# One decoder layer on one core: value products placed next to scores, the last token tile finished in two column halves, the first unit multiplied in order of arrival, stores from two queues

## What is computed

```python
h = rms_norm(x, norm_mix)
cols = h @ w_in                        # 9752 columns: q, k, v of three attentions, and gates
y_a = swa_attention(...)               # window 128, sinks, 8 heads of 64
y_b = stick_breaking(...)              # 4 heads of 128
y_c = nsa_attention(...)               # compressed, selected and window branches, 8 heads of 64
merged = sum(sigmoid(g_i) * (y_i @ w_br_i) for i in (a, b, c))
x = x + merged @ w_out
h = rms_norm(x, norm_ffn)
x = x + (silu(h @ w_gate) * (h @ w_up)) @ w_down    # inner width 5632
out = rms_norm(x, norm_final)
```

## Time and profile before

| | |
|---|---|
| median of three executions | 1398.5 us |
| the profiled execution's own time | 1400.08 us |
| its span | 1398.4 us |
| granted clock of TensorE, mean | 0.998 |
| PE matmul busy | 1386.4 us, 99% |
| PE weight loads busy | 1172.5 us, 84% |
| DVE, ACT, POOL busy | 66%, 50%, 3% |
| DMA | 260.58 MB, 186 GB/s |

### The profile page before, as it was taken

How to read it: one execution, slowest core, us unless ns; L and a number is a source line. 1 busy time by engine, 2 the same in 40 slices (tenths; PEclk the granted TensorE clock), 3 DMA queues, 4 the chain that set the end, 5 groups by cost and what they waited for, 6 DMA issues and landing times.

```text
span 1398.4 us, 18555 instructions
## 1 busy us (share of the span) xinstructions
PE 1386.4 (99%) x7344; PEld 1172.5 (84%) x7344; DVE 923.2 (66%) x1189; ACT 701.9 (50%) x912; POOL 45.4 (3%) x70
## 2 busy tenths in 40 slices
PE   9999999999999999999999999999999999999997
PEld 8999977777788888888888989888888898888886
DVE  5455557657655657666788888874446788887554
ACT  7333356656545655465645555543334455545443
POOL 4000000000000110000000000000000000000111
PEclk9999999999999999999999999999999999999999
DMA  7777755545565667556566665565666575667653
GB/s 239 247 217 219 216 140 150 149 139 148 150 184 164 188 200 213 174 164 201 157 182 204 213 184 177 184 216 193 191 185 179 182 221 164 192 190 228 207 188 115
DMA packets 135233, 260.58 MB, mean 186 GB/s; under 512 B 8448, under 2 KB 25408, under 8 KB 134768
## 3 DMA queue, kind: packets, MB, share of 16 engines
q1 hardware_dynamic: 133328, 251.89, 59.7%
q0 software_dynamic: 1792, 7.57, 1.5%
q10 hardware_dynamic: 32, 0.01, 0.0%
HBM read 257.33 MB, written 2.10 MB: 186 GB/s over the span
## 4 chain that ended last, share of the span: by engine, by line
PE 94%; DVE 3%; DMA 1%; ACT 1%; issue 1%; SPq 0%; ACTq 0%; DVEq 0%
PE bank L628 25%; PE bank L629 25%; PE bank L630 25%; PE bank L867 5%; PE bank L869 5%; PE bank L870 5%; PE bank L619 2%; DVE weight_lo_ring L1259 1%; DMA raw_ring<-in_w_up 1%; PE bank L766 1%; PE bank L677 1%; DVE weight_sums_lo L1279 0%; ACT weight_hi_ring L1029 0%; DMA x<-in_x 0%; DVE weight_sums L1268 0%
## 5 line engine op out<-in xcount | busy, mean ns | idle before, releaser
L1259 DVE TENSOR_TENSOR weight_lo_ring<-raw_ring,weight_hi_ring 128x1024 fp32r<-128x1024 f32 (+2 forms) x480 | 581.3, 1220 | 326.6 <-ACT weight_hi_ring L1029 273.0
L1029 ACT ACTIVATE weight_hi_ring<-raw_ring 128x1024 fp32r<-128x1024 f32 (+2 forms) x432 | 448.7, 1051 | 363.4 <-PE bank L630 297.2
L628 PE MATMUL bank<-weight_hi_ring,hT_hi 128*128 128x512 f32 (+2 forms) x768 | 303.3, 395 | 0.0
L629 PE MATMUL bank<-weight_lo_ring,hT_hi 128*128 128x512 f32 (+2 forms) x768 | 296.9, 387 | 0.0
L630 PE MATMUL bank<-weight_hi_ring,hT_lo 128*128 128x512 f32 (+2 forms) x768 | 296.8, 386 | 0.0
L628 PEld LDWEIGHTS bank<-weight_hi_ring,hT_hi 128*128 128x128 f32 x768 | 145.0, 189 | 31.2 <-issue 6.5
L630 PEld LDWEIGHTS bank<-weight_hi_ring,hT_lo 128*128 128x128 f32 x768 | 145.0, 189 | 27.2
L629 PEld LDWEIGHTS bank<-weight_lo_ring,hT_hi 128*128 128x128 f32 x768 | 145.2, 189 | 24.6
L628 PE MATMUL bank<-weight_hi_ring,h2T_hi 128*128 128x512 f32 x352 | 139.6, 397 | 0.6 <-DVE weight_lo_ring L1259 0.5
L629 PE MATMUL bank<-weight_lo_ring,h2T_hi 128*128 128x512 f32 x352 | 139.1, 395 | 0.0
L628 PE MATMUL bank<-weight_hi_ring,actT_hi 128*128 128x512 f32 x352 | 139.0, 395 | 0.0
(11 more groups left out here) (238 smaller groups left out, 1736.5 us busy)
## 6 DMA issues: line engine op xcount, KB each, us to landing
raw_ring<-in_w_in SPq DMA_DIRECT2D x96, 512.0 KB, 3.6
raw_ring<-in_w_gate SPq DMA_DIRECT2D x88, 512.0 KB, 4.5
raw_ring<-in_w_up SPq DMA_DIRECT2D x88, 512.0 KB, 4.3
raw_ring<-in_w_down SPq DMA_DIRECT2D x88, 512.0 KB, 4.6
raw_ring<-in_w_in SPq DMA_DIRECT2D x56, 452.0 KB, 4.2
raw_ring<-in_w_out SPq DMA_DIRECT2D x32, 512.0 KB, 4.6
raw_ring<-in_w_br_c SPq DMA_DIRECT2D x16, 256.0 KB, 4.7
raw_ring<-in_w_br_a SPq DMA_DIRECT2D x16, 256.0 KB, 7.4
```

The costliest lines, as they stand in the source:

```text
L628: pe.matmul(dst, x_hi, w_hi, start=first and k == 0, stop=False)
L629: pe.matmul(dst, x_hi, w_lo, start=False, stop=False)
L1029: act.activation(whi[:, s, :, 0:width(u)], raw[:, s, :, 0:width(u)], ACT.Copy).then_inc(hi_ready, 1)
L1259: dve.tensor_tensor(lo, w, hi.bitcast(F32), ALU.subtract).then_inc(lo_ready, 1)
```

## The change

Four edits stand in one diff.

- `VALUES_AT` is the scores' slot + 6 instead of + 7, on PE and DVE.
- In the last chunk, tile 1 is multiplied in two halves of 256 columns, each in a bank of its own (3 and 6), in all ten units. In the last four units the order is tile 0, first half of tile 1, second half of tile 1. DVE adds each half by itself, and ACT squares each by itself into its own column of `sumsq`.
- ACT stores the chunks that it scales from its own DMA queue; SP stores those of DVE.
- Unit 0 is multiplied as four high-by-high matmuls, four with the low weights, four with the low activations, each group with its own wait. ACT and DVE take the weights of unit 0 before the transposed piece.

```diff
-VALUES_AT = {soft_slot(i) + 7: i for i in range(N_SOFT)}
+VALUES_AT = {soft_slot(i) + 6: i for i in range(N_SOFT)}
...
             for t in range(TT):
-                for n in range(NC_D // 2):
-                    for name, c in (("dve", DVE_OUT[t][n]), ("act", ACT_OUT[t][n])):
-                        sp.wait_ge(scaled[name], t * NC_D // 2 + n + 1)
-                        sp.dma_start(out_b[:, t, c * W:(c + 1) * W], X[:, t, c * W:(c + 1) * W]).then_inc(stored, 16)
+                for n, c in enumerate(DVE_OUT[t]):
+                    sp.wait_ge(scaled["dve"], t * NC_D // 2 + n + 1)
+                    sp.dma_start(out_b[:, t, c * W:(c + 1) * W], X[:, t, c * W:(c + 1) * W]).then_inc(stored, 16)
...
+            def first_unit():
+
+                pe.wait_ge(t_hi, 1)
+                pe.wait_ge(hi_ready, 1)
+                for r, (x, w) in enumerate(((hT_hi, whi), (hT_hi, wlo), (hT_lo, whi))):
+                    if r == 1:
+                        pe.wait_ge(lo_ready, 1)
+                    if r == 2:
+                        pe.wait_ge(t_lo, 1)
+                    for k in range(UK):
+                        for t in range(TT):
+                            m = pe.matmul(bank[t][:, 0:WQ], x[:, k, t * P:(t + 1) * P], w[:, 0, k, 0:WQ],
+                                          start=r == 0 and k == 0, stop=False)
+                m.then_inc(unit_used, 1)
...
+                    if i == LAST_DOWN:
+                        products(u % RING, (actT_hi, actT_lo), c % 2, j == 0, False, UK * j, tiles=(0,))
+                        for e in range(2):
+                            m = half_products(u, j, e)
+                        m.then_inc(unit_used, 1)
+                        return
...
+            def half_products(u, j, e):
+
+                dst = bank[LAST_HALF[e]][:, 0:Q4]
+                last = j == KD_H[1] - 1
+                for k in range(UK):
+                    x_hi, x_lo = (m[:, UK * j + k, P:S] for m in (actT_hi, actT_lo))
+                    w_hi, w_lo = quarters(u, k, e)
+                    pe.matmul(dst, x_hi, w_hi, start=j == 0 and k == 0, stop=False)
+                    pe.matmul(dst, x_hi, w_lo, start=False, stop=False)
+                    m = pe.matmul(dst, x_lo, w_hi, start=False, stop=last and k == UK - 1)
+                return m
+
             def last_units():
 
                 n = KD_H[1]
-                for t in range(TT):
+                for j in range(n - RING, n):
+                    u = AT["down", LAST_DOWN, j]
+                    pe.wait_ge(lo_ready, u + 1)
+                    m = products(u % RING, (actT_hi, actT_lo), LAST_DOWN[1] % 2, False, j == n - 1, UK * j, tiles=(0,))
+                m.then_inc(tile0_full, 1)
+                for e in range(2):
                     for j in range(n - RING, n):
...
+                        m = half_products(AT["down", LAST_DOWN, j], j, e)
+                        if e == 1:
                             m.then_inc(unit_used, 1)
...
+                    if e == 0:
+                        m.then_inc(last_half_full, 1)
...
             for m in range(UPC):
+                if m == 0:
+                    split(m)
                 hi_of_transposed(m, 4 + m % 4, hT_hi[:, 2 * m:2 * m + 2, :], gainT[:, 0, 2 * m:2 * m + 2])
-                split(m)
+                if m > 0:
+                    split(m)
...
+                for e in range(1 + t):
+                    act.wait_ge(added, TT * (NC_D + c) + t + e + 1)
+                    act.wait_ge(squares, 2 * TT * NC_D + TT * c + t + e)
+                    w = W // (1 + t)
+                    act.activation(bank[7][:, 0:w], X[:, t, c * W + e * w:c * W + (e + 1) * w], ACT.Square,
+                                   accum_out=sumsq[:, t, c + e:c + e + 1]).then_inc(squares, 1)
                 root(3 + t, slice(t, t + 1))
...
+                    act.activation(X[:, t, cols], X[:, t, cols], ACT.Copy, scale=rstd[:, t:t + 1]).then_inc(scaled["act"], 1)
+                    act.wait_ge(scaled["act"], t * NC_D // 2 + n + 1)
+                    act.dma_start(out_b[:, t, cols], X[:, t, cols]).then_inc(stored, 16)
...
+                if (h, c) == LAST_DOWN:
+                    dve.wait_ge(tile0_full, 1)
+                    dve.tensor_tensor(X[:, 0, cols], bank[2 * (c % 2)][:, :], X[:, 0, cols], ALU.add).then_inc(added, 1)
+                    finish(0)
+                    for e in range(2):
+                        dve.wait_ge(last_half_full, 1) if e == 0 else dve.wait_ge(unit_used, v + 1)
+                        half = slice(c * W + e * Q4, c * W + (e + 1) * Q4)
+                        dve.tensor_tensor(X[:, 1, half], bank[LAST_HALF[e]][:, 0:Q4], X[:, 1, half],
+                                          ALU.add).then_inc(added, 1)
+                    finish(1)
+                    return
```

More of the change, by code:

```diff
@@ L121 @@
 LAST_DOWN = (1, NC_D - 1)
+LAST_HALF = (3, 6)
 def is_seven(u):
@@ L253, in build_layer @@
         gainT = place("gains_T", [4, KD])
-        sumsq = place("sumsq", [TT, NC_D])
+        sumsq = place("sumsq", [TT, NC_D + 1])
         stat = place("stat", [6, TT])
@@ L1239, in _ @@
             for t in range(TT):
-                act.wait_ge(added, TT * (NC_D + c) + t + 1)
-                square(t, c, bank[7], 2 * TT * NC_D + TT * c + t)
+                for e in range(1 + t):
[4 more added lines that the diff above has]
+                                   accum_out=sumsq[:, t, c + e:c + e + 1]).then_inc(squares, 1)
                 root(3 + t, slice(t, t + 1))
                 act.wait_ge(rstd_ready, 3 + t)
-                for n in ACT_OUT[t]:
-                    act.wait_ge(gained, n + 1)
-                    piece = X[:, t, n * W:(n + 1) * W]
-                    act.activation(piece, piece, ACT.Copy, scale=rstd[:, t:t + 1]).then_inc(scaled["act"], 1)
+                for n, chunk in enumerate(ACT_OUT[t]):
+                    act.wait_ge(gained, chunk + 1)
+                    cols = slice(chunk * W, (chunk + 1) * W)
+                    act.activation(X[:, t, cols], X[:, t, cols], ACT.Copy, scale=rstd[:, t:t + 1]).then_inc(scaled["act"], 1)
+                    act.wait_ge(scaled["act"], t * NC_D // 2 + n + 1)
+                    act.dma_start(out_b[:, t, cols], X[:, t, cols]).then_inc(stored, 16)
         @block.vector
@@ L1332, in add_down @@
                 cols = slice(c * W, (c + 1) * W)
+                if (h, c) == LAST_DOWN:
[8 more added lines that the diff above has]
+                    finish(1)
+                    return
+                dve.wait_ge(unit_used, v + 1)
                 for t in range(TT):
-                    if (h, c) == LAST_DOWN and t == 0:
-                        dve.wait_ge(tile0_full, 1)
-                    else:
-                        dve.wait_ge(unit_used, v + 1)
                     dve.tensor_tensor(X[:, t, cols], bank[2 * (c % 2) + t][:, :], X[:, t, cols], ALU.add).then_inc(added, 1)
-                    if (h, c) == LAST_DOWN:
-                        finish(t)
             def finish(t):
-                norm(3 + t, 3 * TT * NC_D - TT + t + 1, slice(t, t + 1))
+                norm(3 + t, 3 * TT * NC_D - TT + 2 * t + 1, slice(t, t + 1))
                 dve.wait_ge(rstd_ready, 3 + t)
@@ L1373, in norm @@
                 total, mean, root, y, z = (stat[:, r, tiles] for r in (2, 0, 1, 3, 4))
-                chain(dve.tensor_reduce(out=total, in_=sumsq[:, tiles, :], axis=AX_X, op=ALU.add))
+                n_sums = NC_D + (tiles == slice(1, TT))
+                chain(dve.tensor_reduce(out=total, in_=sumsq[:, tiles, 0:n_sums], axis=AX_X, op=ALU.add))
                 dve.tensor_scalar(mean, total, 1.0 / D, EPS, ALU.mult, ALU.add).then_inc(mean_ready, 1)
```

11 lines of the change are left out of this document (3 added, 8 removed).

## The result

The changed kernel took 1401.49 us (median of 22 executions, 1399.71 to 1403.55), the kernel before 1398.62 us (22 executions, 1397.45 to 1400.74). The ratio is 1.0019, with a 95% interval of 1.0012 to 1.0026: 2.9 us slower, where 1396.4 had been forecast and the range ended at 1398.2.

A forecast was written before the change was run, and what follows sets the result against it. PE was taken as the bound, busy 99% of the span. Values -1.7, start -0.05, halves +0.1 -0.5 and stores +0.1 sum to -2.05 us, from a median of 1398.5 to 1396.4; range 1394.8 to 1398.2.

The forecast's parts named there:

- the rivals: Four cases for the time: middle as summed (chance 0.64), free change of form (0.17), no middle gain (0.14), ACT's queue (0.05).
- ACT's queue: Rival in the tail: slow store issues on ACT make the kernel slower, 1399.9 at an issue of 1.4 us; chance 0.05.
- Values next to scores: Attention stretch on PE: joining eight value groups to scores saves 0.20 us each; with the compressed values -1.7 us, range 0 to 3.3.
- The compressed group: Full-width compressed values in attention, behind scores: they save the scores' return alone, 0.11 us.
- The first unit: Start of PE's work: unit 0 waits for less, but PE's filler queue hides most of it; -0.05 us.
- The 0.11 us at most: Upper bound on the gain before unit 0: last filler started at 8.63, first matmul at 8.74.
- the rate of the first unit's matmuls changes at another time: One of the signs, to be read in the changed profile, that would show the prediction wrong.
- Two halves: Last chunk: 120 matmuls of 256 columns replace 60 of 512, +0.1 us on PE; shorter tail, -0.49; net -0.4.
- The tail: After PE's last matmul: DVE's add 0.69 to 0.42 us, ACT's square 0.60 to 0.38, together -0.49.
- Stores: Last stores from two queues: SP's 0.5 us of queueing goes, but ACT's issue of 0.46 delays its second scaling; +0.1 us.
- no store landed more than 3.5 us after issue: Sign at the end: the last store landing more than 3.5 us after its issue would show the prediction wrong; 3.3 was assumed.

## Why the prediction was wrong

- **The step that failed** is the list of what the change adds. The prediction priced matmuls, adds, squares, waits and stores, and gave the ninth column of `sumsq` no term. It moved the activations by 32 bytes against the weights and cost 5.3 us (1401.49 against 1396.20), twice all that the four edits win. None of the rivals had it either; the one that ended slower, ACT's queue, did not occur. Every price per matmul was taken from rows of before and assumed to hold after; with the addresses moved it did not.
- **Values next to scores** was right: -1.7 predicted, -1.75 measured alone, one change of form per pair (2.33 us for the joined group against 2.32). Scores to values cost what scores to a unit cost: the 0.85 us from the first score to the first value product is the 0.85 from the first score to L628 in the earlier trace rows. "Mode switching requires drain", the Trainium skill says (TensorEngine Tiling (Array Packing), Key Properties). The trace agrees that this change is not free; its size comes from the rows alone. The compressed group saved nothing where 0.11 was assumed.
- **The first unit** was mis-sized: -0.05 predicted, -0.7 measured alone (with an interval up to +0.6). The 0.11 us at most was read from one execution with slow fillers. In an execution where they are fast, PE reached unit 0 earlier than 8.63 and waited; "the rate of the first unit's matmuls changes at another time" was named as what would show the prediction wrong, and it did, but as a gain. It also hid the loss: the profiled execution of after had this 3.0 us head start.
- **Two halves** was mis-sized on PE: from the first matmul of the last chunk to the last is 27.65 us before and 28.11 with the old addresses restored. With the last matmul's own 0.23 and 0.12 that is +0.34, not +0.1: the halves step at 0.118 to 0.119 rather than 0.117, and the rest, under 0.1, is left to the changes of width. The price came from `h2T`, whose distance from the ring is the good one for 256 columns (d = 64); the halves read `actT` at d = 128. The tail gave the 0.49 in full (8.35 us after the last matmul's start for 8.95, less 0.11 for the shorter matmul). Net -0.15, with -0.4 predicted.
- **Stores** came out at 0, with +0.1 predicted. ACT's last issues take 0.34 and not 0.46, and no store landed more than 3.5 us after issue.
- The sum with these sizes: -1.75 - 0.7 - 0.15 = -2.6, and the changed kernel with the old addresses is 1396.20 against 1398.78, -2.6. With +5.3 that is +2.7; measured +2.9. The first two terms are known to about 1.3 us each, so an agreement this close is partly luck, and so is how well 1396.20 meets the forecast: the start gave 0.65 more than predicted and the halves 0.25 less.

## What to carry to other kernels

Where buffers are placed by hand one after another, a few bytes more in a small one move all that follow: print the addresses before and after a change, and count a moved operand as a part of the change. In a kernel that PE bounds, try the distance between moving and stationary operand in steps of 32 or 64 bytes up to 256: here one line took 10.7 us off the kernel before (1387.67), and with the four edits it made 1384.59, 1.0% below before, where the four edits alone had won 0.2%. When equal code runs at another pace, compare the duration's median by kind of matmul; single profiles differ by up to 3 us at the start alone.

## What the runs showed of the hardware

- The start-to-start distance of fp32r matmuls of 512 columns, each with its own 128x128 weight load, depends on the distance in bytes between the two operands in a partition, with a period of 256 bytes: 227 to 229 ns at a multiple of 256, up to 237 for one kind at 160. The pattern is steady: at the 32-byte shift the three products of the down projection take 231, 232 and 237 ns on average, in every kernel that has it. A move of both operands together changes nothing (1399.01 against 1399.14), and what DVE, ACT and the DMA do meanwhile moves the step compared above by 1.4 ns at most. What in the chip makes it, the runs don't tell; other types, and matmuls that share a weight load, were not tried.
- PE's first rate is half, and when it doubles differs between executions of one and the same order: 0.38 us per matmul of 452 columns up to 12.9 us in one profile, up to 10.0 in another. The trace's record of the granted clock begins at that moment (12.94 and 9.96), and the steps before it are those seen at a recorded 0.50.
- A change between full width and 64 rows or 64 columns costs PE 0.09 to 0.11 us; 64 rows followed by 64 columns cost one such change (2.33 us for the joined group).
- A DMA issue of 256 KB takes ACT 0.34 us (once 0.37), and SP 0.45 (four in 1.80).
